# Delta-rule scan of a hybrid denoising step: block solves moved into the pairs, solved blocks loaded compactly and spread by GpSimd, join and inverse on four quarters of the array

## The reference, cut to what matters

```python
def rwkv_scan(s0, r, w, a, b, k, v):
    def step(s, inp):
        r_t, w_t, a_t, b_t, k_t, v_t = inp
        sa = jnp.einsum('bdhvk,bdhk->bdhv', s, a_t)
        s = s * w_t[..., None, :] + sa[..., None] * b_t[..., None, :] + v_t[..., None] * k_t[..., None, :]
        return s, jnp.einsum('bdhvk,bdhk->bdhv', s, r_t)
    s_fin, y = lax.scan(step, s0, (r, w, a, b, k, v))
    return y, s_fin
```

## Time and profile before

| | us |
|---|---|
| runs | 2644.72, 2644.95, 2647.1 (median 2644.95) |
| profiled execution, its own time | 2641.31 |
| its span, first to last instruction | 2639.5 |
| PE busy / PE weight loads busy | 2414.8 / 1987.1 |
| DVE / ACT / POOL busy | 1323.3 / 721.4 / 604.3 |
| mean granted PE clock | 0.973 |

### The profile page before, as it was taken

How to read it: one execution, slowest core, us unless ns; L and a number is a source line. 1 busy time by engine, 2 the same in 40 slices (tenths; PEclk the granted TensorE clock), 3 DMA queues, 4 the chain that set the end, 5 groups by cost and what they waited for, 6 DMA issues and landing times.

```text
span 2639.5 us, 50736 instructions
## 1 busy us (share of the span) xinstructions
PE 2414.8 (91%) x21498; PEld 1987.1 (75%) x21498; DVE 1323.3 (50%) x2166; ACT 721.4 (27%) x1179; POOL 604.3 (23%) x244
## 2 busy tenths in 40 slices
PE   2799999999999996777889999899999999999997
PEld 2677778788887775777855578788888888888885
DVE  7665657528467776553453332643334334333335
ACT  3272644634455443323310000310001100010002
POOL 0320120111111111000000044244434433443441
PEclk9899999999999997989989999899999999999999
DMA  6313111021467775565422321011011111111102
GB/s 243 100 52 110 44 66 59 27 108 62 125 197 195 186 211 149 144 181 130 125 98 103 109 92 41 16 40 41 33 40 41 34 39 41 41 32 41 40 33 88
DMA packets 259489, 234.53 MB, mean 89 GB/s; under 512 B 189218, under 2 KB 213922, under 8 KB 258466
## 3 DMA queue, kind: packets, MB, share of 16 engines
q1 hardware_dynamic: 259362, 232.70, 28.8%
HBM read 173.79 MB, written 57.02 MB: 87 GB/s over the span
## 4 chain that ended last, share of the span: by engine, by line
PE 72%; SPq 9%; DVE 8%; DMA 4%; issue 4%; ACT 2%; POOL 1%; DVEq 0%; ACTq 0%; POOLq 0%
PE PS L837 18%; PE PS L839 18%; PE PS L838 18%; PE PS L1256 5%; SPq L704 4%; PE PS L946 3%; SPq L664 2%; PE PS L918 2%; PE PS L960 1%; PE PS L932 1%; DMA buffer<-ops_kept 1%; DVE buffer L1933 1%; PE PS L920 1%; DMA buffer<-solved_kept 1%; DVE buffer L1932 1%
## 5 line engine op out<-in xcount | busy, mean ns | idle before, releaser
L837 PE MATMUL PS<-buffer,buffer 128*128 128x512 f32 (+1 forms) x2784 | 1007.3, 362 | 19.8 <-POOL buffer L2194 8.3
L839 PE MATMUL PS<-buffer,buffer 128*128 128x512 f32 (+1 forms) x2784 | 998.0, 358 | 0.0
L838 PE MATMUL PS<-buffer,buffer 128*128 128x512 f32 (+1 forms) x2784 | 997.9, 358 | 0.0
L837 PEld LDWEIGHTS PS<-buffer,buffer 128*128 128x128 f32 x2784 | 527.2, 189 | 113.5 <-issue 17.7
L839 PEld LDWEIGHTS PS<-buffer,buffer 128*128 128x128 f32 x2784 | 527.2, 189 | 83.3
L838 PEld LDWEIGHTS PS<-buffer,buffer 128*128 128x128 f32 x2784 | 527.6, 189 | 82.3 <-issue 1.1
L2203 POOL TENSOR_TENSOR buffer<-buffer,buffer 128x1024 fp32r<-128x1024 f32 x76 | 184.1, 2423 | 1133.7 <-PE PS L839 526.8
L2150 DVE SCALAR_TENSOR_TENSOR buffer<-PS,buffer,buffer 128x512 f32<-128x512 f32 (+1 forms) x264 | 158.5, 656 | 154.8 <-PE PS L839 154.8
L2204 POOL TENSOR_TENSOR buffer<-buffer,buffer 128x1024 fp32r<-128x1024 f32 x76 | 193.5, 2546 | 6.0
L2126 DVE TENSOR_SCALAR buffer<-buffer,buffer 128x1281 f32<-128x1281 f32 x22 | 34.5, 1567 | 291.0 <-ACT buffer L1690 291.0
L1690 ACT ACTIVATE buffer<-PS 128x512 f32<-128x512 f32 (+1 forms) x66 | 30.0, 529 | 513.0 <-PE PS L839 513.0
(11 more groups left out here) (212 smaller groups left out, 2796.4 us busy)
## 6 DMA issues: line engine op xcount, KB each, us to landing
buffer<-in_w_up SPq DMA_DIRECT2D x44, 512.0 KB, 3.3
buffer<-in_w_in SPq DMA_DIRECT2D x42, 512.0 KB, 5.0
ops_kept<-buffer SPq DMA_DIRECT2D x40, 512.0 KB, 5.9
buffer<-ops_kept SPq DMA_DIRECT2D x80, 256.0 KB, 3.7
buffer<-in_w_ada SPq DMA_DIRECT2D x32, 512.0 KB, 7.2
buffer<-rkv_kept SPq DMA_DIRECT2D x120, 128.0 KB, 3.4
buffer<-in_w_down SPq DMA_DIRECT2D x22, 512.0 KB, 3.2
buffer<-in_x SPq DMA_DIRECT2D x20, 512.0 KB, 9.8
```

The source lines that it names most:

```text
L837: mm(out, w_hi, x_hi, start=start, stop=False)
L838: mm(out, w_hi, x_lo, start=False, stop=False)
L839: return mm(out, w_lo, x_hi, start=False, stop=stop)
```

## The change

- **Solves.** Only batches 0 to 2 are solved during the tiles. Batches 3 and 4 are solved in pairs 0 to 6 and 8 to 14 at five rows a pair; SP stores them after its loads for pairs 7 and 15 and loads the blocks of batch 4 behind the first of these.
- **`store_solved`.** 32 DMAs in place of 16, each from 8 partitions in place of 16, so that both 32x32 blocks of a head's half lie side by side in DRAM.
- **`load_solved`.** Two DMAs of 128 KB a pair into one of two compact tiles (`solved`), in place of 16 into `DX`. They wait only for the spreading two pairs back. Pairs 0 and 1 are loaded before the loop.
- **`expand` on POOL.** Two `tensor_tensor` a pair multiply the compact tile, broadcast along the rows, by the mask `near` into `DX`; it waits for `q_done` of the pair before. The clearing of `DX` goes; the clearing of `ya` now stands behind `expand(0)`, and DVE waits for it before its pair 0.
- **r, k, v** come back in twelve DMAs of 640 KB, one a pair behind the loads for pairs 2 to 13.
- **`joined` and `inverse`** write to banks 6 and 7 and use all four quarters of the array; `Z` and the copy of `Q` follow.
- **DVE.** The four masks of the second grams become two of twice the size, and the second far mask moves behind `Z`.
- **`outputs_of_tokens`** takes its products in another order.

```diff
-        SOLVE_SLOT = [(15 + 4 * b, 17 + 4 * b) for b in range(NBATCH - 1)]
+        SOLVE_SLOT = [(15 + 4 * b, 17 + 4 * b) for b in range(NBATCH - 2)]
+        SOLVE_FROM, SOLVED_BY = (0, 8), (7, 15)
...
-                            dst = dram["solved_kept"][d, HB * q:HB * q + HB, kind, at:at + NX * HB]
-                            sp.dma_start(dst.rearrange("s (x t) -> x s t", t=HB), src[d * 64 + q * NX:d * 64 + (q + 1) * NX]) \
-                                .then_inc(solved_out, 16)
+                            for e in range(2):
+                                row = HB * (q if kind == 1 or e == 0 else q ^ 2)
+                                dst = dram["solved_kept"][d, row:row + HB, kind, at:at + NX * HB].rearrange("s (x e t) -> e x s t", e=2, t=HB)
+                                sp.dma_start(dst[e], src[d * 64 + q * NX + e:d * 64 + (q + 1) * NX:2]).then_inc(solved_out, 16)
...
+                if i == 0:
+                    sp.wait_ge(code_done, 2 * NG_UNITS)
+                elif i == 1:
+                    sp.wait_ge(w_used, len(TILES))
+                else:
+                    sp.wait_ge(dx_ready, i - 1)
+                sp.wait_ge(solved_out, 512 * (i // 4 + 1))
                 if i >= 1:
-                    sp.wait_ge(q_done, i)
-                else:
-                    sp.wait_ge(cleared, 4)
-                sp.wait_ge(solved_out, 256 * (i // 4 + 1))
+                    sp.wait_ge(solved_in, 32 * i)
                 for d in range(2):
-                    n = chunk_at(d, i) // C
-                    for q in range(4):
-                        dst = DX[HB * q:HB * q + HB, :, d * NP:(d + 1) * NP, HB * (q % 2):HB * (q % 2) + HB]
-                        for kind in range(2):
-                            sp.dma_start(dst[:, kind], dram["solved_kept"][d, HB * q:HB * q + HB, kind, n * NP * HB:(n + 1) * NP * HB]
-                                         .rearrange("s (j t) -> s j t", t=HB)).then_inc(dx_in, 16)
+                    n = chunk_at(d, i) // C * NP * HB
+                    sp.dma_start(solved[i % 2][:, :, d * NP:(d + 1) * NP, :].rearrange("p k j t -> p k (j t)"),
+                                 dram["solved_kept"][d, :, :, n:n + NP * HB]).then_inc(solved_in, 16)
...
-            load_solved(0)
             for i in range(1, NC):
+                load_solved(i)
                 load_grams(i)
                 load_keys_b(i)
                 load_values(i)
-                load_solved(i)
...
-                if i in (3, 5, 7):
-                    n = (i - 3) // 2
-                    sp.dma_start(rkv[:, 4 * n:4 * n + 4, :], kept[:, 4 * n:4 * n + 4, :]).then_inc(state_in, 16)
-                if i == 9:
-                    store_solved(NBATCH - 1)
+                if 2 <= i < 14:
+                    sp.dma_start(rkv[:, i - 2, :], kept[:, i - 2, :]).then_inc(state_in, 16)
+                if i in SOLVED_BY:
+                    store_solved(NBATCH - 2 + SOLVED_BY.index(i))
+                    if i == SOLVED_BY[0]:
+                        load_blocks(NBATCH - 1)
...
-                hold((far_out, after), (s_ready, after), (dx_in, blocks))
-                products(7, GB[:, 0], DX[:, 1]).then_inc(lz_done, 1)
+                hold((far_out, after), (s_ready, after), (dx_ready, after))
+                if first:
+                    pe.wait_ge(st_read, 1)
+                joined().then_inc(lz_done, 1)
...
-                products(7, Z, DX[:, 0]).then_inc(q_done, 1)
+                inverse().then_inc(q_done, 1)
...
-                mask_gram(2, GB, gram_far, 1, gb_out)
                 dve.wait_ge(gk_done, i + 1)
-                mask_gram(4, GK, gram_mask, 0, None)
-                mask_gram(4, GK, gram_mask, 1, gk_out)
+                mask_both(4, GK, gram_mask, gk_out)
                 dve.wait_ge(lz_done, i + 1)
-                tt(Z, PS[:, 7, :].rearrange("p (j t) -> p j t", t=C), eye.unsqueeze(1).to_broadcast([P, 2 * NP, C]),
-                   ALU.add).then_inc(lz_ready, 1)
+                tt(by_parity(Z), two_banks(6), eye.unsqueeze(1).unsqueeze(1).to_broadcast([P, 2, NP, C]), ALU.add).then_inc(lz_ready, 1)
+                mask_one(2, GB, gram_far, 1, gb_out)
...
+            def expand(i):
+
+                pool.wait_ge(solved_in, 32 * (i + 1))
+                if i >= 1:
+                    pool.wait_ge(q_done, i)
+                for kind in (1, 0):
+                    ins = pool.tensor_tensor(DX[:, kind].rearrange("p j (b t) -> p j b t", t=HB),
+                                             solved[i % 2][:, kind].unsqueeze(2).to_broadcast([P, 2 * NP, 2, HB]),
+                                             near.unsqueeze(1).to_broadcast([P, 2 * NP, 2, HB]), ALU.mult)
+                    if kind == 1:
+                        G.step(ins)
+                    else:
+                        ins.then_inc(dx_ready, 1)
...
-            pool.memset(DX, 0.0).then_inc(cleared, 1)
+            expand(0)
             pool.wait_ge(w_used, len(TILES))
             pool.memset(ya[:, :, :], 0.0).then_inc(cleared, 1)
+            for i in range(1, NC):
+                expand(i)
```

More of the change, by code:

```diff
@@ L356, in build @@
         assert g3.at + NX * C // 2 <= RING
+        wk = Space(UPPER + T)
+        S = wk(2 * NP, C)
+        solved = [wk(2, 2 * NP, HB)]
+        DX = wk(2, 2 * NP, C)
+        assert wk.at <= RING
         wk = Space(FREE)
@@ L721, in _ @@
                     store_blocks((t - 2 - UNIT_SLOT[0]) // 2)
-                for b in range(NBATCH - 1):
+                for b in range(NBATCH - 2):
                     if t == SOLVE_SLOT[b][1] + 1:
                         store_solved(b)
-                if t - 3 in UNIT_SLOT and (t - 3 - UNIT_SLOT[0]) // 2 % 2 == 1:
+                if t == 30:
+                    load_solved(0)
+                if t - 3 in UNIT_SLOT and t < 30 and (t - 3 - UNIT_SLOT[0]) // 2 % 2 == 1:
                     load_blocks((t - 3 - UNIT_SLOT[0]) // 4)
@@ L1127, in state_update, with joined, inverse @@
                                      skip_group_check=True)
+                return ins
+            def joined():
+                for j in range(2 * NP):
+                    for h in range(2):
+                        f, t = halves(j, h)
+                        ins = mm(at_bank(STATE_BANK, j)[f], GB[t, 0, j, :], DX[t, 1, j, :], start=True, stop=True)
+                return ins
+            def inverse():
+                for j in range(2 * NP):
+                    for h in range(2):
+                        f, t = halves(j, h)
+                        ins = mm(at_bank(STATE_BANK, j)[t], Z[f, j, :], DX[f, 0, j, :], start=True, stop=True)
                 return ins
@@ L1150, in hold, with turn @@
                     pe.wait_ge(sem, value)
-            def turn(i, after, twice, loads, blocks, first=False):
+            def turn(i, after, twice, loads, first=False):
                 if not first:
@@ L1187, in _ @@
             state_turned(6, lambda j: SI[:, j, :]).then_inc(st_turned, 1)
-            turn(0, 1, 0, 32, 256, first=True)
-            pe.wait_ge(st_read, 1)
+            turn(0, 1, 0, 32, first=True)
             with ExitStack() as counts:
-                after, twice, loads, blocks = (counts.enter_context(pe.register(n)) for n in ("after", "twice", "loads", "blocks"))
+                after, twice, loads = (counts.enter_context(pe.register(n)) for n in ("after", "twice", "loads"))
                 with pe.Fori(1, NC) as i:
@@ L1195, in _ @@
                     pe.reg_mul(loads, after, 32)
-                    pe.reg_mul(blocks, after, 256)
-                    turn(i, after, twice, loads, blocks)
+                    turn(i, after, twice, loads)
             pe.wait_ge(rh_out, NC)
@@ L1698, in ffn_values @@
                 act.activation(factH[:, slot, :], fact[:, slot, :], ACT.Copy).then_inc(fact_rounded, 1)
-            act.wait_ge(cleared, 6)
+            act.wait_ge(cleared, 5)
             ffn_values(0, 0, 1)
@@ L1964, in _, with mask_one @@
             dve.wait_ge(s_ready, 1)
-            def mask_gram(b, dst, mask, a, last):
+            def mask_one(b, dst, mask, a, done):
                 for e in range(2):
@@ L1970, in mask_gram, with mask_both @@
                              mask[:, :, a, :], ALU.mult)
-                    if e == 0 or last is None:
+                    if e == 0:
                         V.step(ins)
                     else:
-                        ins.then_inc(last, 1)
+                        ins.then_inc(done, 1)
+            def mask_both(b, dst, mask, done):
+                for e in range(2):
+                    ins = tt(dst[:, :, e:2 * NP:2, :].rearrange("p a k t -> p k a t"),
+                             PS[:, b + e, :].rearrange("p (k a t) -> p k a t", a=2, t=C), mask, ALU.mult)
+                    if e == 0:
+                        V.step(ins)
+                    else:
+                        ins.then_inc(done, 1)
             def dve_y(n):
@@ L2160, in ffn_turn @@
                 ffn_values(i, 1, 0)
```

(2 more changed lines are left out.)

53 lines of the change are left out of this document (27 added, 26 removed).

## The result

| | before | after |
|---|---|---|
| median (lowest to highest) | 2646.49 (2644.72 to 2648.78) | 2656.03 (2650.47 to 2657.08) |
| profiled execution / its span | 2641.31 / 2639.5 | 2657.03 / 2655.2 |
| mean granted PE clock | 0.973 | 0.965 |

The changed kernel is slower by little, but clear of none: ratio 1.0034, interval [1.0024, 1.0044], some 9.5 us. The forecast was 12.9 us faster. The two profiled executions lie 15.7 us apart, because that of before is 5.2 us under its median; what follows accounts for their traces.

A forecast was written before the change was run, and what follows sets the result against it. It read the chain of waits, PE holding 72%, with SP's sixteen issues inside the scan's pair loop. Terms -24.0 - 13.8 - 36.1 + 36 + 16 + 9 = -12.9 us took 2641.31 to 2628.4 (2632.0 against the median); range 2606 to 2672.

The forecast's parts named there:

- three stores in the tiles: Stores of solved blocks left in the projection tiles: 3 us more each, between 1.5 and 11.5, +9 us.
- start of the scan: Solved blocks load right behind the last gate tile, so the first join starts at 1036.5 instead of 1050.34: -13.8 us.
- pair period: Scan pairs without SP's loop of sixteen issues take 11.0 us in place of 12.2: -24.0 us for twenty pairs.
- early stalls: Waits of the scan's early pairs, behind big loads and the store of batch 4, all go: -36.1 us.
- two new stores in the scan: Stores of batches 3 and 4, 16 us of issues each, stall PE at the first grams 16.4 and 15.6: +36 us.
- DVE and POOL: POOL's spread holds DVE's solve rows, making ten pairs with five long rows longer: +16 us, between 0 and 24.
- eight partitions, eight engines: Rival for the stores: each halved DMA takes as long as a whole one before, 38 us more, 2670; chance 0.2.
- gives some 0.3 back: In a pair, right sides wait for the far mask moved behind `Z`, returning some 0.3 of the inverse's 0.4 us saving.
- what I wrote of SP's spare time: Early stalls: r, k, v pieces of a quarter size, issued when SP has 8 us to spare, should hide.
- the sign: Whole kernel: faster, by 12.9 us; chances faster 0.51, slower 0.33, same 0.16.

The follow-up runs named there:

- b_rows: The kernel before with each of a store's 16 DMAs of solved blocks cut in two by rows, still on 16 partitions: 2674.44 us, ratio 1.0106.
- a_rkv3: The changed kernel with r, k and v back in three DMAs of 2560 KB in place of twelve: 2656.27 us, ratio 1.0034.
- a_late: The changed kernel with SP issuing the next grams and keys before the solved blocks behind each store in the scan: 2646.25 us, ratio 0.999.
- a_whole: The changed kernel with the stores of before, 16 DMAs of 16 partitions, and halves swapped by the loads: 2612.64 us, ratio 0.9871.
- p_best: The changed kernel with 4 KB store runs scattered by loads, `ya` cleared first, and grams and keys ahead of solved blocks behind scan stores: 2574.77 us, ratio 0.9724.

## Why the prediction was wrong

By its steps, us in the traces of before and after, from the tiles to the last join (1318.26 before, 1330.18 after, 11.9 later; 19 periods lie between first and last join, where the forecast counted twenty):

| step | forecast | measured |
|---|---|---|
| three stores in the tiles | +9 | +32.3 |
| start of the scan | -13.8 | -12.9 |
| pair period | -24.0 | -31.7 |
| early stalls | -36.1 | -28.3 |
| two new stores in the scan | +36 | +45.5 |
| DVE and POOL | +16 | +7.0 |
| sum | -12.9 | +11.9 |

- **The step that failed is the price of a store DMA.** I took 32 issues at 0.5 us, "since the halved DMA asks less of the queue". Halving the pieces on the same partitions does that: `b_rows` has the 0.50 us and 16 us that I took. But the change halves the partitions, and then an issue stays at 0.68 and a store at 21.8. The rival *eight partitions, eight engines* named this, its point of decision (0.60 us) and a total of +38 on the forecast; the stores came out 23.3 + 9.5 = 32.8 above it. I gave it 0.2 because landing had stayed at 2.9 us, which says nothing of how long an issue holds the queue.
- **The tiles were mis-sized on their own.** I let 3 of each store's microseconds through, and 8 more for the rival. Measured: 25.16 against 13.52 us for the first store, 32.1 more for the three, and 32.3 more at the last gate store. `b_rows` says the same, its longer stores arrive whole. ACT's operands stand behind the store on the one queue, and PE had no slack to lose.
- **The pair** was better than forecast, 1.67 us in place of 1.2. I had written that the moved mask "gives some 0.3 back" and the state update starts as late as before; it starts 7.5 to 7.6 us behind the join (1188.55 to 1196.01, 1309.06 to 1316.64) where it was 8.33. The late pairs bear the mechanism out: SP's loop and the wait for `Z` are gone, and putting the quarters or the order back costs 0.5 to 0.7.
- **The early stalls.** The mechanism was half right. The stalls behind the big loads went, but not by cutting these (`a_rkv3`): what I wrote of SP's spare time bears it out, the cutting doesn't. The first two periods stay long (15.0 and 13.8 us, 7.8 over 2 x 10.53; they were long before), which I had counted as gone.
- **The stores in the scan**, step by step from J, the join of pair 6 (1144.16): the store began at J+4.8 (I had 6.9), took 21.8 (16), landed in 1.9 (2.9), grams were issued at J+30.3 (27.1), product 6.8 later (6.4). The wait was 20.4 (16.4), and of the two long periods 2.3 and 2.7 more went behind the wait, where I had 2 for slower products. The order of issues behind the store adds 3.6 of the wait (`a_late`).
- **DVE and POOL.** Rows fed from SBUF are held until POOL's instruction ends, as read from the earlier trace rows. I took all rows at the median of 0.36 and the full 2.6 us as held. In most spreads two instructions lose 0.9 to 1.1 each, and the first and last rows of a solve take 0.2. Long pairs came out at 10.5 to 12.2, 7.0 in all over 10.53.
- **The start** held: 13.4 us from the last gate store to the first join, with `ya` as its last link (the 9.56 us of PE wait on DVE, DVE 26.65 on POOL).

The remaining 3.8 us between the traces lie behind the last join. PE has 6438 instructions there in both, busy for 1279.6 us at a mean granted clock of 0.97 where it was 1274.5 at 0.98. What lowered the clock isn't shown; runs of the kernel before spread over more than that (2638.32 to 2655.14).

The range of 2606 to 2672 held the time; the sign didn't. In the traces the forecast is 24.8 us off (-12.9 to +11.9): 32.8 from the stores, less 8.0 from all other steps. With 16 full-width stores the same change brings some 34 us (`a_whole`, 0.9871, with other loads too); cut over half the partitions they take it all back.

## What to carry to other kernels

Before you cut a DMA in pieces, ask which size gets smaller: here half the pieces on the same 16 partitions made it cheaper, half the partitions hardly did (0.50 and 0.65 to 0.68 us in place of 0.69). Where a transfer must be scattered, put the scatter where the queue has time: the same 128-byte pieces cost 22 us in one stall as stores and 4.7 us a pair as loads, hidden in the undisturbed pairs but not right behind a store (`p_best`). A store on the only queue is paid nearly in full by whoever loads behind it (25.9 of 28 us in `b_rows`), and a microsecond taken out of a pair elsewhere can be given back at the next such stall.

## What the runs showed of the hardware

- The issue of a DMA with pieces of 128 B on SP's queue, by pieces and partitions, in the scan: 512 on 16 partitions 0.69 us, 256 on 16 0.50, 256 on 8 0.65 to 0.68; 16 runs of 4 KB on 16 partitions 0.46. With 32 pieces to a partition it is 0.65 to 0.69 in each case. By their packets of 4 B the DMAs from 16 partitions run on 16 engines and those from 8 on 8.
- POOL instructions of 1.3 us hold a DVE row with both inputs in SBUF for their full length: 1.30 and 1.29 us in place of 0.35, 21.9 us over a scan. The Trainium skill says so too (SBUF — State Buffer, "SBUF: two separate sides": whichever starts first gets the pair of ports for the whole instruction, the other fully blocks), and the rows agree.
- While PE waits for a store its granted clock falls. In the changed kernel it was at 1.00 from 1155 to 1160 with PE at work; PE was idle from 1165 to 1181 at 0.50 (1.2 GHz), and the first 4 us of work behind it ran at 0.50 too. There the 32 products of the first grams take 1.99 us against 1.08 to 1.09 in an undisturbed pair. The two stretches, columns as above:

```profile
1165.00:1181.00 16.00, 0.00 (x0) 0.00 (x0) 0.00 (x0) 1.06 (x1) 2.49 (x2) 0.50 0.56 158
1181.00:1185.00 4.00, 3.79 (x109) 3.82 (x113) 0.79 (x3) 0.00 (x0) 0.00 (x0) 0.50 0.60 206
```
